# The modulation weights of a two-block transformer kernel: a queue of their own, a transposed layout, and weight splits as wide as a pair

## What is computed

```python
silu_c = jax.nn.silu(c)
mod = silu_c @ w_ada[l] + b_ada[l]
shift_m, scale_m, gate_m, shift_f, scale_f, gate_f = jnp.split(mod, N_MOD, axis=-1)
h = modulate(rmsnorm(x, g_norm_mix[l]), shift_m, scale_m)
proj = h @ w_in[l]
...
x = x + gate_m[:, None, :] * mix
h = modulate(rmsnorm(x, g_norm_ffn[l]), shift_f, scale_f)
f = jnp.square(jax.nn.relu(h @ w_ff1[l])) @ w_ff2[l]
x = x + gate_f[:, None, :] * f
```

## Time and profile before

| what | us |
|---|---|
| median of 3 runs (lowest, highest) | 2245.44 (2241.61, 2247.24) |
| profiled execution | 2245.16 |
| its span | 2243.4 |
| busy: PE, DVE, ACT, POOL | 2031.7, 1451.5, 1060.7, 214.1 |

### The profile page before, as it was taken

One profiled execution on the slowest core, in us unless ns is written; L12 is line 12 of the kernel. 1 busy time (PEld: TensorE's weight loads), 2 busy tenths in 40 slices (PEclk: granted clock), 3 DMA queues, 4 the chain that ended last, 5 costly groups with the idle time before them and its releaser, 6 DMA issues. The chain is left out here.

```text
span 2243.4 us, 26960 instructions
## 1 busy us (share of the span) xinstructions
PE 2031.7 (91%) x9432; PEld 1678.2 (75%) x9432; DVE 1451.5 (65%) x2623; ACT 1060.7 (47%) x2120; POOL 214.1 (10%) x247
## 2 busy tenths in 40 slices
PE   5668868976879999999999999988999999999999
PEld 4457756755767788888888877977988887888877
DVE  6888777766878765556565555577666656556554
ACT  4344444553454444544544555555544445444443
POOL 0110033400100010010011013020001001001000
PEclk9788988988989999999999999998999999999999
DMA  8778877626868755556555555633544355565554
GB/s 317 242 247 304 284 256 253 232 85 242 269 237 308 255 197 179 194 181 195 180 189 186 188 190 162 212 112 106 154 142 144 115 168 198 184 193 187 190 188 158
DMA packets 129129, 450.01 MB, mean 201 GB/s; under 512 B 14304, under 2 KB 14560, under 8 KB 128352
## 3 DMA queue, kind: packets, MB, share of 16 engines
q1 hardware_dynamic: 126016, 435.84, 59.1%
q0 software_dynamic: 1856, 9.44, 1.2%
q10 hardware_dynamic: 1120, 3.01, 0.4%
HBM read 444.03 MB, written 4.19 MB: 200 GB/s over the span
## 5 line engine op out<-in xcount | busy, mean ns | idle before, releaser
L270 DVE TENSOR_TENSOR wlo<-raw,whi 128x512 fp32r<-128x512 f32 (+4 forms) x1336 | 895.9, 704 | 515.0 <-ACT whi L269 493.6
L269 ACT ACTIVATE whi<-raw 128x512 fp32r<-128x512 f32 (+4 forms) x1336 | 773.0, 605 | 776.9 <-PE g L361 482.0
L359 PE MATMUL g<-whi,lhsA_hi 128*128 128x512 f32 (+4 forms) x1840 | 718.0, 390 | 39.7 <-DVE wlo L270 29.7
L361 PE MATMUL g<-whi,lhsA_lo 128*128 128x512 f32 (+4 forms) x1840 | 698.0, 379 | 0.0
L360 PE MATMUL g<-wlo,lhsA_hi 128*128 128x512 f32 (+4 forms) x1840 | 697.4, 379 | 0.0
L359 PEld LDWEIGHTS g<-whi,lhsA_hi 128*128 128x128 f32 x1840 | 355.6, 193 | 110.4 <-DVE wlo L270 43.4
L361 PEld LDWEIGHTS g<-whi,lhsA_lo 128*128 128x128 f32 x1840 | 354.5, 193 | 57.0
L360 PEld LDWEIGHTS g<-wlo,lhsA_hi 128*128 128x128 f32 x1840 | 355.7, 193 | 52.4 <-issue 1.0
L525 DVE SCALAR_TENSOR_TENSOR acc<-raw,small,acc 128x512 f32<-128x512 f32 x360 | 278.4, 773 | 34.1 <-DMA raw<-in_w_ada 15.0
L359 PE MATMUL g<-whi,lhsF_hi 128*128 128x512 f32 x512 | 203.8, 398 | 0.4 <-DVE wlo L270 0.4
L360 PE MATMUL g<-wlo,lhsF_hi 128*128 128x512 f32 x512 | 202.2, 395 | 0.0
(11 more groups left out here) (291 smaller groups left out, 1640.5 us busy)
## 6 DMA issues: line engine op xcount, KB each, us to landing
raw<-in_w_ff SPq DMA_DIRECT2D x256, 512.0 KB, 4.3
raw<-in_w_ada SPq DMA_DIRECT2D x192, 512.0 KB, 4.7
raw<-in_w_in SPq DMA_DIRECT2D x176, 512.0 KB, 4.3
raw<-in_w_out SPq DMA_DIRECT2D x64, 512.0 KB, 4.4
raw<-in_w_in SPq DMA_DIRECT2D x80, 384.0 KB, 3.3
raw<-in_w_mem_kv SPq DMA_DIRECT2D x16, 512.0 KB, 5.1
raw<-in_w_branch_a SPq DMA_DIRECT2D x12, 512.0 KB, 3.7
raw<-in_w_branch_b SPq DMA_DIRECT2D x12, 512.0 KB, 3.5
```

The lines of the kernel that those rows point to most:

```text
L269: t_hi = AC.put(lambda e, x=x, hi=hi: e.activation(hi, x, ACT.Copy), landed[j], free)
L270: t_lo = DV.put(lambda e, x=x, hi=hi, lo=lo: e.tensor_tensor(lo, x, hi.bitcast(F32), ALU.subtract), landed[j], t_hi, free)
L359: PE.put(lambda e, o=o, x=xh, w=h, f=first: e.matmul(o, x, w, start=f, stop=False), w, mark=False)
L361: tok = PE.put(lambda e, o=o, x=xl, w=h, f=last: e.matmul(o, x, w, start=False, stop=f), mark=t == 1)
```

## The change

The 192 modulation blocks leave `plan` and stand in a queue of their own, `adas`. `Queue` keeps an expected clock for each engine (`due`, `us`). `pump` calls `fill`, which appends modulation blocks while the expected landing and DVE time plus 1.3 lie before PE's expected clock. What is not done when it is needed is appended at once: `modulated` names its chunks in `wanted`, and `run` then calls `ada_token`, which appends blocks until the chunk is complete; `gate` does so for the gates. In `u_mem` two blocks stand behind each pair.

`w_ada` is given transposed: a block is 128 output columns by 1024 of the depth. DVE multiplies it with silu(c), held in each partition in `srow`, and sums along the row in the same instruction (L526 of the changed kernel), so that the sums over the partitions by PE go away. The gates, which are needed along the row, are spread by four small DVE instructions and one fp32 matmul for each chunk (`spread`).

The two units of memory keys and values use the fp32 weights and activations as they are (`native`), without splits. For all others both halves of a pair are split by one instruction on each engine, the hi products of a pair (8) stand ahead of the lo products (4), there are 5 raw slots and 4 split slots of a pair each, and splits are put in 4 pairs ahead. The rows of x are scaled by ACT in eight pieces instead of by POOL in two. The kernel also loads c along the row and gives a smaller scratch to the descriptors that POOL writes.

```diff
-NRAW, NSPLIT = 4, 7
+NRAW, NSPLIT = 5, 4
...
+def across(w):
+    return np.ascontiguousarray(w.T.reshape(6 * D // P, P, 2, D // 2).transpose(0, 2, 1, 3))
...
+    def expect(self, waits, us):
+        self.t = max([self.t] + [self.due.get((id(s), v), 0.0) for s, v in waits]) + us
+        return self.t
...
-    whi = sb("whi", [P, NSPLIT, 512], F32R)
-    wlo = sb("wlo", [P, NSPLIT, 512], F32R)
+    whi = sb("whi", [P, NSPLIT, 1024], F32R)
+    wlo = sb("wlo", [P, NSPLIT, 1024], F32R)
...
     def consume():
...
+        src, n, native = plan[j]
         state["split"] += 1
+        i, x, landed = fetch(src, n)
+        if native:
+            halves[j] = (i, x, landed)
+            return
...
+        hi, lo = whi[:, s % NSPLIT, 0:2 * n], wlo[:, s % NSPLIT, 0:2 * n]
+        t_hi = AC.put(lambda e: e.activation(hi, x, ACT.Copy), landed, free, us=0.2 + n * 0.00167)
+        t_lo = DV.put(lambda e: e.tensor_tensor(lo, x, hi.bitcast(F32), ALU.subtract), landed, t_hi, free,
+                      us=0.15 + n * 0.00208)
...
+    def ada_next():
+        c, k0 = adas.popleft()
+        i, x, landed = fetch(a["w_ada"][4 * c + k0 // 4, k0 // 2 % 2], 512)
+        raw_free[i] = [ada_part(x, landed, c, k0)]
+
+    def fill():
+
+        while adas:
+            i = state["slot"] % NRAW
+            if raw_free[i] is None:
+                break
+            issue = max([SP.t] + [due[id(q), v] for q, v in raw_free[i]])
+            landed = max(issue, due.get("dma", 0.0)) + 1.55 + 2.0
+            if max(DV.t, landed) + 1.3 > PE.t:
+                break
+            ada_next()
...
         for _ in range(n):
+            fill()
...
-            consume_to(ahead_of(j))
+            consume_to(j + (2 if plan[j][2] else 4))
             pair = u["pairs"][i] + u["k_off"] // 2
             while lhs.ready[pair] is None:
                 pump(1, 3)
+                for c in wanted.pop(pair, ()):
+                    ada_token(c)
...
+            for kk, t in steps_of:
...
+                w = [t_hi, lhs.ready[pair]] + (gfree[par] if first else [])
+                PE.put(lambda e, o=o, x=xh, w=h, f=first: e.matmul(o, x, w, start=f, stop=False), w, mark=False, us=us)
+                PE.put(lambda e, o=o, x=xl, w=h: e.matmul(o, x, w, start=False, stop=False), mark=False, us=us)
+            for kk, t in steps_of:
...
+                tok = PE.put(lambda e, o=o, x=xh, w=l, f=end and kk == 1: e.matmul(o, x, w, start=False, stop=f), t_lo,
...
+    for cs in ([0, 4, 1, 5], [2, 6, 3, 7], [8, 9, 10, 11], [12, 16, 13, 17, 14, 18, 15, 19], [20, 21, 22, 23]):
+        adas.extend((c, k0) for c in cs for k0 in range(0, 16, 2))
...
+        b.tok = DV.put(lambda e: e.scalar_tensor_tensor(
+            out=src, in0=src, scalar=0.5, in1=sv, op0=ALU.mult, op1=ALU.mult, accum_out=b.ap[:, i:i + 1]),
+            t_in, ready_c["silu"], b.free, us=1.3)
...
     def ada_token(c):
         while c not in ada_done:
-            ada_reduce(*sums_due.popleft()[1])
+            ada_next()
         return ada_done[c]
...
+            for m in range(4):
+                t = DV.put(lambda e, m=m, q=16 * g + 4 * j + m: e.tensor_scalar(rot[m], ident, gcols[:, q:q + 1], None,
+                                                                              ALU.mult), ada_done[c], t_cst, used_)
...
+            tok = PE.put(lambda e, T=T: e.matmul(T.ap[:, :], ones, rot_all[:, :], start=True, stop=True), t, T.free, us=0.9)
...
+    def gate(g, j):
+        ada_token(8 + 12 * g + j)
+        while (g, j) not in gate_done:
+            pump(1, 6)
+        return gate_done[g, j]
...
-            for t in range(2):
-                t_of["xs"] = PO.put(lambda e, t=t: e.tensor_scalar(xs[:, t, :], xs[:, t, :], rx[:, t:t + 1], None,
-                                                                   ALU.mult), t_of["rx"])
+            for q in range(4):
+                for t in range(2):
+                    xc = xs[:, t, 512 * q:512 * q + 512]
+                    t_of["xs", q] = AC.put(lambda e, t=t, xc=xc: e.activation(xc, xc, ACT.Copy, scale=rx[:, t:t + 1]),
+                                           t_of["rx"])
...
-    par, tok = run(u_mem[0], width=3)
+    par, tok = run(u_mem[0], width=3, adas_per_pair=2)
...
         cs = [4 * sec + (sec // 2) * 4 + j // 2, 4 * sec + (sec // 2) * 4 + 4 + j // 2]
+        wanted[j] = cs
...
-        add_in(run(u_out[j]) if j else first_out, j, gt, True, lambda j=j: ada_token(8 + j))
+        add_in(run(u_out[j]) if j else first_out, j, gt, True, lambda j=j: gate(0, j))
...
-            add_in(run(u_f2[4 * g + j], width=3), j, gt, g == 3, lambda j=j: ada_token(20 + j))
+            add_in(run(u_f2[4 * g + j], width=3), j, gt, g == 3, lambda j=j: gate(1, j))
```

More of the change, by code:

```diff
@@ L256, in consume, with fetch @@
+    halves, read = {}, {}
+    def fetch(src, n):
+        i = state["slot"] % NRAW
+        state["slot"] += 1
+        x, free = raw[:, i, 0:2 * n], raw_free[i]
+        assert free is not None
+        raw_free[i] = None
+        return i, x, SP.dma(x, src, raw_sem[i], free, us=n * 0.00303)
     def consume():
         j = state["split"]
[L259 to L276, removed]
@@ L329, in need, with run @@
             yield
[L331 removed]
+    def run(u, steps=1, width=2, adas_per_pair=0):
         par = state["unit"] % 2
@@ new lines, in run @@
+            steps_of = [(kk, t) for kk in range(2) for t in range(2)]
+            end = i == len(u["tiles"]) - 1
+            if plan[j][2]:
+                slot, x, landed = halves[j]
+                for kk, t in steps_of:
+                    o, xt = G[2 * par + t][:, 0:n], lhs.hi[:, 2 * pair + kk, t * P:t * P + P]
+                    w = x[:, kk * n:kk * n + n]
+                    first = i == 0 and kk == 0
+                    waits = [landed, lhs.ready[pair]] + (gfree[par] if first else [])
+                    tok = PE.put(lambda e, o=o, xt=xt, w=w, f=first, z=end and kk == 1: e.matmul(o, xt, w, start=f, stop=z),
+                                 waits, mark=kk == t == 1, us=n * 0.00168)
+                raw_free[slot] = [tok]
+                for _ in range(adas_per_pair):
+                    ada_next()
+                pump(steps, width)
+                continue
@@ L400, in split_from @@
             sc = scales[i]
-            th = AC.put(lambda e, o=hi, s=src, c=sc: e.activation(o, s, ACT.Copy, scale=c), tok, lhs.free, *extra)
-        for i in range(n_k):
+            th = tl = AC.put(lambda e, o=hi, s=src, c=sc: e.activation(o, s, ACT.Copy, scale=c), tok, lhs.free, *extra)
+        for i in range(n_k if lhs.lo is not None else 0):
             src = bank.ap[:, 256 * i:256 * i + 256]
@@ L428, in build, with mix @@
     lhs_q, lhs_kv, lhs_f, lhs_y = (Lhs(None, None, n) for n in (4, 2, 16, 16))
-    def mix(us, adas, later=0, row=0):
+    def mix(us, row=0, native=False, later=0):
         built = []
-        total = sum((k[1] if isinstance(k, tuple) else k) // 2 for *_, k, _ in us)
-        at = done = 0
         for w, c0, n, K, lhs in us:
@@ new lines, in ada_reduce, with spread @@
+        ada_done[c] = t
+    gate_done = {}
+    def spread(g, free):
+        used_ = [PO.tok()]
+        for j in range(4):
+            c = 8 + 12 * g + j
+            wanted["gate"] = [c]
+            while c not in ada_done:
+                yield
+            for m in range(4):
+                t = DV.put(lambda e, m=m, q=16 * g + 4 * j + m: e.tensor_scalar(rot[m], ident, gcols[:, q:q + 1], None,
+                                                                              ALU.mult), ada_done[c], t_cst, used_)
+            yield
+            T = yield from grab(TB)
+            tok = PE.put(lambda e, T=T: e.matmul(T.ap[:, :], ones, rot_all[:, :], start=True, stop=True), t, T.free, us=0.9)
+            used_ = [tok]
+            yield
+            dst = gt[:, 512 * j:512 * j + 512]
+            gate_done[g, j] = AC.put(lambda e, T=T, dst=dst: e.activation(dst, T.ap[:, :], ACT.Copy), tok, free)
+            T.release([gate_done[g, j]])
@@ L728, in build @@
     lam()
-    par, tok = run(u_mem[1])
+    par, tok = run(u_mem[1], adas_per_pair=2)
     t_of["mv"] = evac2(par, tok, 512, mv, t_of["rm"], scale=(rm[:, 0:1], rm[:, 1:2]))
-    consume_to(state["split"] + 1)
-    for c in (0, 4, 1, 5):
-        ada_token(c)
-    while "xs" not in t_of:
+    while ("xs", 3) not in t_of:
         pump()
@@ L1178, in build @@
     k_rr = k
-    for c in range(12, 20):
-        ada_token(c)
     for jc in range(4):
         bg.append(chunk(jc))
-    gate_bias[5] = load(PO, gt[:, :], a["b_ada"][0:1, 5 * D:6 * D].to_broadcast([P, D]), [DV.tok()])
+    bg.append(spread(1, [DV.tok()]))
     ssg = sm(8)
```

243 lines of the change are left out of this document (96 added, 147 removed).

## The result

The changed kernel takes 2367.9 us (median of 4 runs, 2366.0 to 2371.4) against 2244.7 before (median of 4 runs): a ratio of 1.0551, 95% interval 1.0531 to 1.0571. That is +121 us where +83 were forecast. Slower was right; the time lies 3 us above the forecast's own range of 2290 to 2365, at the very end of the whole range (2368), in the rival that expected a larger loss. The profiled execution is 2366.0 us.

The account below looks back on a forecast made before the run. PE was taken to bound the kernel from 758.9 us on; before, what counts is whether modulation blocks spread over PE's work or stand before it. -19 + 11 - 15 - 12 + 123 - 5 = +83 gave 2328 us, range 2272 to 2368.

Parts of the forecast that it names:

- the rival that expected a larger loss: Whole kernel: transfers at 1.80 us a block, longer half clock, wide splits blocking attention's short steps; 2365 to 2390 us, chance 0.10.
- stage 5: First feed-forward group, 214.7 us before: rows of modulation blocks leave PE idle; +123 us.
- Stages 1 to 4: Start and memory units -19 us, half and latent units +11, ten attention steps -15, tail and output units -12.
- stage 3: Ten steps with attention, 180.6 us before: some 18 blocks instead of about 44, half of 30 idle us gained; -15 us.
- Half units: Six product units after the memory units: no modulation stands in them, 65 us of PE instead of 98.3, 10.8 us apart.
- Units two to four of `u_f1`: Later units of the first feed-forward products: 22.8 us each instead of 27.3; -14 us.
- the four units `u_f2`: Second feed-forward products: 4, 8, 8 and 8 blocks between the first units, with restarts of PE; +51 us.
- 18 x 1.6 = 28.8 us of transfers ... PE works 5.4 in each: First unit `u_f1`: each of three further quarters has 16 modulation and 2 product blocks, set by transfers; unit +86 us.
- stage 6: Rest of the kernel, no modulation, bound by PE: wider splits unload DVE but stand longer before small steps; -5 us.
- stage 1: Start and memory units, 132.4 us before: transfers of 27.3 MB set the time, PE's fp32 matmuls hide; -19 us.
- stages 2 to 4: Half and latent units +11 us, ten attention steps -15, attention tail and output units -12.
- is excluded by the order itself: Feed-forward part: the expected clock cannot fill PE's gaps so that nothing is forced, as 64 blocks stand in the last possible place.

Follow-up runs that it names:

- e5: Against the changed kernel: splits put in 3 pairs ahead instead of 4, in the first unit `u_f1` alone, no block moved; 2339.2 us.
- e6: Against the changed kernel: splits put in 3 pairs ahead instead of 4 everywhere, rule of `fill` untouched; 2242.2 us.
- e3: Against the changed kernel: a margin of 3 us in the rule of `fill`, so blocks may end up to 3 us behind PE's expected clock; 2204.5 us.

## Why the prediction was right and wrong

**Right.** The mechanism, and its places. The blocks stood in rows, and stage 5 took all that the early stages gave. Stages 1 to 4 came to -33 together, forecast -35, though the share of stage 3 (-20, forecast -15) was half of the idle time by choice, so its closeness is in part luck. Half units are 10.9 us apart, forecast 10.8. Units two to four of `u_f1` take 68.2 us, forecast 68.4. With the gates' blocks the four units `u_f2` take 143.2 us against 89.9 between the same evacuations, +53 for a forecast of +51.

**The failed step.** It is in stage 5: "18 x 1.6 = 28.8 us of transfers ... PE works 5.4 in each". PE's pairs were costed as hidden beside the blocks. The first unit was to end after 36 + 3 x 28.8 + 5.4 = 128 us. It took 31.6 until PE starts (633.74), 3 x 34.1, and 13.3 for the last two pairs: 147.3. The term for the start was 4 too high, the quarters 16 too low, the last pairs 8 too low. The two pairs are mostly at half clock, and a split between them needs the slot that the first gives back; in DVE's queue that split stands ahead of the next slice and the next blocks. e5 shows it: without that one dependence, and with every block in place, the 28.3 us of DVE's wait go, and the quarter is 26.4 us, though its granted clock is still 0.69. The order had been read for where the blocks stand, not for which split slot the instruction between them waits for.

**The second, smaller one** is stage 6: -5 forecast, +8.8 measured. The growth is in the stretch with the attentions (742.4 to 750.9 us). The prediction saw wide splits only as load taken off DVE and as a longer turn in its queue. The runs showed slower POOL instructions beside them: in that stretch PE waited 10.4 and 3.6 us for POOL's `row` and `y` lines before, and 14.4 and 5.2 after, 5.6 of the 8.5. They also showed 14 us less in stage 6 when both widths are cut; of that, what lies beyond POOL's part has no shown cause.

For the second the Trainium skill has a rule that speaks against this change: SBUF — State Buffer, SBUF: two separate sides, has VectorE operations with two SBUF inputs and GpSimd operations that read SBUF take a shared pair of ports by turns, each for its whole instruction. By that rule a low split twice as long holds POOL up longer, and the trace agrees (1.07 and 1.40 us); that it is this port, no run isolates.

**The rival that came true** in size, "the same with transfers at 1.80 us a block, longer half clock, and wide splits", did so largely by luck. It had 11 us more in stage 5, 10 in stage 1, up to 20 in stages 2 to 4 and 20 in stage 6; measured against the forecast it was 22, 1.5, nothing in sum and 14. Transfers were not a reason: 365 GB/s behind 610.72, 1.47 us a block in e5. The half clock made each pair longer, but it cost the quarters only through the dependence on the split slot, which this rival did not name. Only wide splits were a reason of their own, in stage 6.

The statement that a fill by the clock "is excluded by the order itself" was right, but had no reason. e6 and the sum of prices beside it give it: the look-ahead equal to the number of slots ties DVE's expected clock to PE's. e3 shows that a margin in the rule lifts the same bar.

## What to carry to other kernels

When blocks of background work stand in an engine's queue, read not only how many there are, but what the foreground instructions between them wait for: one that needs a buffer that the consumer gives back only now puts both in series. A look-ahead as deep as its ring of buffers contains such a wait, and it can also tell a planner that there is no room; one less gave 126 us here. Doubling the width of an instruction saves its fixed part on its own engine, and can be paid for on another engine, here POOL, on which the consumer waits.

## What was not expected of the hardware

POOL's two-input fp32 instruction of 128x384 (and two other forms, L702 before, L720 after) goes from 1073 to 1399 ns on average when DVE's instructions beside it are 1024 instead of 512 elements long, though DVE is busy for less in all (449.7 us of that stretch before, 416.9 after). A multiply of 1024 elements with the sum along the row is followed at the next start after 1.15 us, its record being 1.22. The low split of 1024 elements, which has no sum, is followed after 1.14 (640.47 to 641.61), so the sum adds a record of 0.08 us and no time that shows. And cutting ACT's rounding alone in two gives nothing (2368.6 us), while cutting it together with the low split gives 15 us over the low split alone; the cause of these 15 is open.
